# A weight stream of 340 slots: raw buffers dropped, each transfer landing in the ring itself

## The reference

```
# first_block, layer a
h = rms_norm(x, a_norm) @ a_w_in              -> q, k, v, qm, gate
q, k = rope(rms_norm per head of 64)
o  = diff_attention(q, k, v, lam)             # softmax(c=0) - lam * softmax(c=1), 6 heads, causal
om = memory_attention(qm, mem)                # 4 heads over 256 memory rows
x  = x + (cat[rms_norm(o), om] * silu(gate)) @ a_w_out
# first_block, layer b
k, v = split(rms_norm(x, kv_norm) @ w_kv_shared);  q, qm, gate from b_w_in
o  = stick_breaking_attention(q, k, v)        # sigmoids and a running product, 12 heads
x  = x + (cat[o, om] * silu(gate)) @ b_w_out
# second_block, twice
u, v, z_a, c_q, c_kv, k_rope, z_b, x_c, z_c, g_a, g_b, g_c = split(rmsnorm(x) @ w_in)
y_a = gmlp_spatial(u, layernorm(v)) * silu(z_a)
y_b = mla_attention(c_q, c_kv, k_rope) * silu(z_b)          # 8 heads
y_c = rg_lru(conv(x_c)) * silu(z_c)
merged = sig(g_a) * (y_a @ wa) + sig(g_b) * (y_b @ wb) + sig(g_c) * (y_c @ wc)
x = x + rmsnorm(merged @ w_out)
```

## Time and profile before

| | us |
|---|---|
| time, median of 3 runs (2293.51 to 2296.84) | 2294.11 |
| the profiled execution | 2295.78 |
| its span, first to last instruction | 2294.0 |
| PE busy | 2199.1 (96%) |
| DVE busy | 1192.2 (52%) |
| POOL busy | 1151.6 (50%) |
| ACT busy | 936.4 (41%) |

### The profile page before, as it was taken

One profiled execution on the slowest core, in us unless ns is written; L12 is line 12 of the kernel. 1 busy time (PEld: TensorE's weight loads), 2 busy tenths in 40 slices (PEclk: granted clock), 3 DMA queues, 4 the chain that ended last, 5 costly groups with the idle time before them and its releaser, 6 DMA issues.

```text
span 2294.0 us, 27438 instructions
## 1 busy us (share of the span) xinstructions
PE 2199.1 (96%) x10006; PEld 1694.0 (74%) x10006; DVE 1192.2 (52%) x1827; ACT 936.4 (41%) x1591; POOL 1151.6 (50%) x1360
## 2 busy tenths in 40 slices
PE   7999989999899999999999999799999999999998
PEld 5776567775587668888887888576678888877786
DVE  6877875458668341053248843564420432298442
ACT  4546742356444542232234622344532322237322
POOL 4553245642175224565566765263145665575752
PEclk9999999999999999999999999899999999999999
DMA  4222122321132114322232233122133332332321
GB/s 150 78 83 65 38 82 75 110 65 38 37 101 84 55 47 129 101 92 92 83 101 85 90 102 101 55 84 64 35 104 99 94 101 85 93 100 74 110 92 65
DMA packets 53127, 191.45 MB, mean 83 GB/s; under 512 B 6016, under 2 KB 6400, under 8 KB 52480
## 3 DMA queue, kind: packets, MB, share of 16 engines
q1 hardware_dynamic: 51696, 184.44, 25.7%
q10 hardware_dynamic: 1296, 5.24, 0.7%
HBM read 187.56 MB, written 2.10 MB: 83 GB/s over the span
## 4 chain that ended last, share of the span: by engine, by line
PE 76%; DVE 14%; ACT 4%; POOL 2%; issue 2%; DMA 1%; SPq 0%; DVEq 0%; ACTq 0%
PE proj L554 19%; PE proj L556 19%; PE proj L555 19%; PE score L550 4%; PE proj L550 3%; PE stat L550 2%; POOL lower L506 2%; PE turned L550 2%; DVE small L1825 2%; PE mix L550 2%; DVE tmp L1714 1%; PE score L556 1%; PE score L555 1%; PE score L554 1%; DVE h L1719 1%
## 5 line engine op out<-in xcount | busy, mean ns | idle before, releaser
L506 POOL TENSOR_TENSOR lower<-raw_ring,upper 128x256 fp32r<-128x256 f32 x1340 | 1134.9, 881 | 1087.9 <-ACT upper L1214 1087.9
L554 PE MATMUL proj<-h,upper 128*128 128x512 f32 x1424 | 575.5, 404 | 12.7 <-ACT sq L1318 3.1
L1214 ACT ACTIVATE upper<-raw_ring 128x1024 fp32r<-128x1024 f32 x335 | 350.9, 1058 | 529.5 <-PE proj L554 287.8
L556 PE MATMUL proj<-h,lower 128*128 128x512 f32 x1424 | 556.4, 391 | 0.0
L555 PE MATMUL proj<-h,upper 128*128 128x512 f32 x1424 | 555.6, 390 | 0.0
L554 PEld LDWEIGHTS proj<-h,upper 128*128 128x128 f32 x1424 | 268.1, 188 | 77.5 <-issue 5.7
L556 PEld LDWEIGHTS proj<-h,lower 128*128 128x128 f32 x1424 | 267.6, 188 | 57.0
L555 PEld LDWEIGHTS proj<-h,upper 128*128 128x128 f32 x1424 | 268.2, 188 | 51.3 <-issue 1.9
L554 PE MATMUL proj<-y,upper 128*128 128x512 f32 x586 | 234.1, 399 | 13.1 <-ACT qk L1318 5.9
L555 PE MATMUL proj<-y,upper 128*128 128x512 f32 x586 | 229.5, 392 | 0.0
L556 PE MATMUL proj<-y,lower 128*128 128x512 f32 x586 | 229.5, 392 | 0.0
(11 more groups left out here) (461 smaller groups left out, 3494.2 us busy)
## 6 DMA issues: line engine op xcount, KB each, us to landing
raw_ring<-stream SPq DMA_DIRECT2D x335, 512.0 KB, 3.5
landing<-stream SPq DMA_DIRECT2D x5, 512.0 KB, 10.0
x<-x_in SPq DMA_DIRECT2D x4, 512.0 KB, 6.8
rows<-rows_in ACTq DMA_DIRECT2D x2, 1024.0 KB, 5.2
out<-x SPq DMA_DIRECT2D x8, 256.0 KB, 2.5
memraw<-mem_in SPq DMA_DIRECT2D x1, 1024.0 KB, 13.2
memraw<-mem_in ACTq DMA_DIRECT2D x1, 1024.0 KB, 4.8
rot<-tables_in ACTq DMA_DIRECT2D x2, 512.0 KB, 3.2
```

Of the source, the lines that this page charges most:

```text
L506: ins = nc.gpsimd.tensor_tensor(lower[:, p % RING, a:b], slot_source(p)[:, a:b], upper[:, p % RING, a:b].bitcast(FP32), ALU.subtract)
L554: first_ = nc.tensor.matmul(o, lhsT[0], rhs[0], start=start, stop=False)
L556: return first_, nc.tensor.matmul(o, lhsT[1], rhs[0], start=False, stop=stop)
L1214: nc.scalar.activation(upper[:, p % RING, :], slot_source(p), ACT.Copy).then_inc(split_upper, 1)
```

## The change

`raw_ring` and RAWS go. The room (two slots) is given to the rings: `upper` and `lower` have six slots in place of five. Every slot p now lands in `lower[:, p % 6, :]` (named `landing`). SP waits, before it issues slot p, until slot p-6 has been used up; before, it waited for POOL to be done with slot p-2. ACT no longer waits for `slots_used` itself, only for the landing, and copies from the lower half to the upper half; POOL subtracts in place.

```
-RAWS, RING = 2, 5
+RING = 6
...
-    raw_ring = sb("raw_ring", [P, RAWS, SLOT])
     upper = sb("upper", [P, RING, SLOT], FP32R)
     lower = sb("lower", [P, RING, SLOT], FP32R)
     landing = place("landing", cursor[0] - RING * SLOT, [P, RING, SLOT])
...
     def slot_source(p):
-        return landing[:, p, :] if p < RING else raw_ring[:, (p - RING) % RAWS, :]
+        return landing[:, p % RING, :]
     def slot_arrival(p):
-        return (landed[p], 16) if p < RING else (arrived[(p - RING) % RAWS], 16 * ((p - RING) // RAWS + 1))
+        return landed[p % RING], 16 * (p // RING + 1)
...
         for p in range(RING, SLOTS):
-            if p >= RING + RAWS:
-                sp.wait_ge(*slot_ready(p - RAWS))
-            sp.dma_start(slot_source(p), stream[p, :, :]).then_inc(arrived[(p - RING) % RAWS], 16)
+            sp.wait_ge(slots_used, p + 1 - RING)
+            sp.dma_start(slot_source(p), stream[p, :, :]).then_inc(landed[p % RING], 16)
...
             for p in range(fed[0], min(upto, SLOTS)):
                 act.wait_ge(*slot_arrival(p))
-                if p >= RING:
-                    act.wait_ge(slots_used, p + 1 - RING)
                 nc.scalar.activation(upper[:, p % RING, :], slot_source(p), ACT.Copy).then_inc(split_upper, 1)
```

More of the change, by code:

```diff
@@ L300, in build @@
     split_lower = nc.alloc_semaphore("split_lower")
-    arrived = [nc.alloc_semaphore(f"slot_arrived{r}") for r in range(RAWS)]
     landed = [nc.alloc_semaphore(f"slot_landed{p}") for p in range(RING)]
```

## The result

The changed kernel takes 2347.20 us, median of 4 runs (2346.43 to 2348.83), against 2293.86 us for the kernel before (4 runs, 2293.51 to 2296.84): a ratio of 1.0231, 95% interval 1.0218 to 1.0244. It is slower by 53 us. The forecast was 2336, range 2314 to 2350.

What follows compares the result with a forecast made beforehand. PE, busy 96% of the span, was taken to bound the kernel. Losses of 46.7 us less gains of 5.1 gave 41.6 net, hence 2337.4 on the profiled execution and a forecast of 2336 us, range 2314 to 2350.

Steps and rivals of the forecast that it cites:

- The mechanism: Transfer issued at the slot's release, so 80 copies on ACT start up to 3.5 us later, delaying ACT's work behind them.
- the sixth slot gives the copy no head start: In ACT's list the copy is now the next slot's, needing the same release as before; up to 3.5 us later.
- The plain projections: Plain stretches of projections: 3.5 + 1.06 is 4.6, covered by a job ending over 5.2 us after release; cost nothing.
- the differential tiles: Differential attention: square behind the copy comes later, PE's sum loses 2.2 us in each of four tiles; stage total 14.35.
- the fifth: Fifth differential attention tile: square moves from 273.15 to 276.65 and PE's sum loses 3.15 us.
- the three stick-breaking tiles alike: Stick-breaking attention: later sigmoid delays DVE's product, 3.0 us reaching PE in each of three tiles, 9.0; stage total 12.75.
- The rivals: Paid back in attention tiles, 2308.6 (0.10); landing hardly seen (0.06); gain alone, 2289 (0.08); above 2350 (0.06).
- The gains: Shorter ACT waits for raw-buffer transfers give back 5.1 us where PE waited behind them; bounds nothing and 12.
- After the recurrent unit: At 1311.88 ACT's wait for a transfer goes, and PE's wait for the square: 1.7 in both later layers, 3.4 us.
- The gain of 0.7 that I had put at 340: Between 320 and 341 ACT waits for transfers three times; PE waits 6.81 for DVE's x, so only 0.7 us gained.
- The start: First copy out of the raw ring, at 46.18, starts at 48.6 with a take directly behind it: 2.4 us lost.
- The layer norm: Gated unit's layer norm: takes behind the copy move 3.5, DVE's chain ends later, PE's product waits 2.1 per layer, 4.2.

Runs made afterwards that it cites:

- experiment 1: Changed kernel with every later feed on ACT asking for one slot less, so each transfer starts one release ahead of its copy: 2288.82 us, ratio 0.998.
- experiment 2: Kernel before, with SP also waiting until slot p-5 is used up before it issues slot p; nothing lands in place: 2361.28 us, ratio 1.0297.
- experiment 3: Kernel before with SP's additional wait for slot p-5, and each transfer from the eighth slot on bringing only half its columns: 2331.03 us.
- experiment 5: Changed kernel with SP first landing a slot's first 16 columns, then issuing the whole slot, so the landing is later: 2465.13 us.
- Experiments 4 and 6: Changed kernel asking one slot less only behind the attention stages' transposed-probability copies, 2307.67 us; and one slot less everywhere except those copies, 2328.03 us.

## Why the prediction was right, and where it was off

**The mechanism held.** A transfer issued at the release, a copy that waits for it, and ACT's own work behind the copy: experiment 1 removes it and 58 us go, experiment 2 adds it to the kernel before and 68 come (some of them from the waits for POOL named there), experiments 3 and 5 turn it down and up. That the sixth slot gives the copy no head start, since the copy keeps its place in ACT's list, was the step that decided the sign; experiment 1 shows the same slot at work once the list is told to lag.

**The places held.** Experiments 4 and 6 split the loss into the attention tiles and the rest, and the two parts, 39.2 and 18.9 us above experiment 1, make up 58.1 of the changed kernel's 58.4. The plain projections lost nothing at a landing of 3.5 us. In the differential tiles PE's sum behind the square came 1.95 to 2.06 later where 2.2 was forecast, and 3.25 in the fifth for 3.15; in the three stick-breaking tiles alike the delay that reached PE was 2.5 to 2.7 where 3.0 was. The rivals are out: little was paid back in the tiles, and 264 copies saw the landing.

**The gains held in sum, though not each.** After the recurrent unit 3.5 came where 3.4 was forecast. Between 298 and 388 it was 2.6 for 1.7: the queries after the second memory keys gained 4.1, more than I had given them, and 1.4 was lost ahead of them. Of the 4.1, some 2 are the clock: the windows give 0.91 over 370 to 388 in the trace of before and 1.00 over the same matmuls (399 to 413) in the changed kernel. The other 2.1 is PE's wait for POOL there, gone whole, where I had left 1.0 of it. The gain of 0.7 that I had put at 340 did not come.

**The term that was missing is the clock.** The measured shift is 51.0 and the sum was 41.6. PE's busy time rose by 14.4 us, from 2199.1 to 2213.5, for the same matmuls, and by the mean granted clock the core lost 0.017 x 2344.6 = 39.9 us in place of 0.011 x 2294.0 = 25.2, that is 14.6 more. I had forecast the same clock and the same busy time. By stage, in windows over the four attention stages (the row's third number from the end is the granted clock), of the kernel before:

```profile
208.00:298.00 90.00, 85.40 (x416) 51.26 (x417) 74.82 (x193) 63.65 (x173) 21.16 (x28) 1.00 0.16 47
513.00:628.00 115.00, 104.17 (x556) 62.31 (x555) 90.09 (x162) 65.88 (x171) 29.70 (x32) 0.99 0.13 41
723.00:808.00 85.00, 80.30 (x363) 55.99 (x362) 33.64 (x87) 41.77 (x88) 27.11 (x37) 0.98 0.20 62
1508.00:1608.00 100.00, 97.93 (x429) 71.19 (x428) 53.43 (x97) 49.42 (x94) 52.46 (x62) 1.00 0.28 85
```

The same four stages in the trace of the changed kernel:

```profile
216.00:327.00 111.00, 91.03 (x422) 53.52 (x421) 73.05 (x194) 63.57 (x174) 19.73 (x28) 0.97 0.09 29
538.00:668.00 130.00, 109.20 (x555) 63.99 (x554) 90.25 (x162) 66.44 (x174) 31.78 (x32) 0.95 0.10 29
765.00:854.00 89.00, 79.91 (x359) 55.27 (x358) 32.05 (x88) 41.58 (x88) 26.72 (x38) 0.98 0.17 53
1555.00:1661.00 106.00, 100.12 (x423) 71.57 (x423) 54.58 (x97) 48.80 (x94) 53.78 (x62) 0.97 0.23 69
```

In tiles where PE now stood still more often, the granted clock was at its lower level, 1.2 in place of 2.4 GHz, for a part of the time: 3% of 111 us is 3.3 us in the differential stage, some 5% of 130 us less 1% of 115 in the stick-breaking one 5.4, and 3.2 in the fourth layer's attention. Without it these stages would have lost 16.4, 9.6 and 3.5 where the sum had 14.35, 12.75 and 5.05. PE's idle time between the same matmuls grew by 15.4, 10.0 and 3.8 there. So my waits alone came out about 5 us too high in all (36.6 measured without the clock's 14.4), and the clock more than made up for it. That the lower clock goes with the stalls, and is no accident of one run, is borne out by all 4 runs of the changed kernel (0.979 to 0.983, where those of the kernel before have 0.987 to 0.990), by experiment 1 at 0.986 to 0.988 and by experiment 5 at 0.965 to 0.967. How much of each stage's loss is the clock's was only read from these windows, which are rounded to 0.01; no run holds the clock fixed.

**The smaller misses.** The start cost 4.0 for 2.4, of which the clock is part (1.00 before and 0.94 after, in windows over that stretch). The stretch of k in layer a, 1.65, I had at nothing; it holds no new idle time of PE, and the granted clock was 0.96 before and 0.92 after. In the differential stage I had left out PE's waits for the take of `yf`, which grew from 0.8 us to 2.8 in four. The layer norm cost 1.4 per layer for 2.1, since PE's product waited 0.90 and not 2: I had set the end of DVE's chain against the first of the eight matmuls with `gv`, and only the last two needed it. The price of a late landing was taken as linear in the range by halves of a microsecond; experiments 2 and 3 give 30.3 us for 0.9 us of landing, where 25 places would give 22, but 11.7 of the 30.3 are PE's busy time, so the waiting alone came to 18.6. The limit of 4.2 us for the plain projections was too strict: experiment 5, at 5.1, shows hardly any of them losing.

**Landing time and overlap.** The Trainium skill's fit for the other issuing path ("DMA: Bandwidth & Descriptors", section "Anatomy of one DMA — SWDGE (gpsimd) path") gave an estimate of 3.2 us for the landing; the trace after has 3.5 for 340 transfers, so the row decides. For 8 KB, in experiment 5, the page of the profile shows 1.6 us, and for 256 KB, in experiment 3, 2.6. The Trainium skill, "Trainium Kernel Development and Optimization", section "Best Practices", says to double-buffer so that transfer and compute overlap. Taking the buffers away cost 53 us here, as that rule would have it; but experiment 1 has the overlap back without them, by starting the transfer a release ahead of the copy, which takes up the sixth slot of the ring.

## What to carry to other kernels

When a buffer between a transfer and its consumer goes, ask which event starts the transfer now and where in the in-order list its consumer stands; if both hang on the same event, the whole landing time stands ahead of everything behind that consumer, however idle the engine is on average. A slot more in the ring helped only once the consumer's list was told to lag behind it: here the same memory gave +53 us without the lag and -4.5 us with it. And stalls put into PE's stream can cost more than their length: here 36.6 us of them came with 14.4 us of longer matmuls, while the mean granted clock went from 0.989 to 0.983.

## What the hardware showed that was not expected

In two of the traces one DVE instruction took many times its usual length while POOL ran without a break. From experiment 1, DVE and POOL:

```profile
421.65 10.41 DVE L1709 SCALAR_TENSOR_TENSOR tmp<-x,fcol,gate 128x512 f32<-128x512 f32 x1 [18.53 <-PE score L553]
432.10 0.87 DVE L1713 CAST h<-tmp 128x512 fp32r<-128x512 f32 x1
...
417.52 13.99 POOL L503 TENSOR_TENSOR lower<-landing,upper 128x256 fp32r<-128x256 f32 x20 [8.47 <-ACT upper L1209]
```

And from the changed kernel:

```profile
422.98 14.00 POOL L503 TENSOR_TENSOR lower<-landing,upper 128x256 fp32r<-128x256 f32 x20 [11.05 <-ACT upper L1209]
...
429.52 7.74 DVE L1701 TENSOR_TENSOR half_var<-half_var,std 128x256 f32<-128x256 f32 x1 [12.71 <-ACT std L1278]
437.30 0.42 DVE L1702 TENSOR_TENSOR half_var<-half_var,std 128x256 f32<-128x256 f32 x1
```

The first of these operations takes 0.75 to 1.11 us elsewhere in that stretch; here it ended half a microsecond after POOL's row of 20 subtractions, and the second, 0.42 long where it is repeated, ended 0.3 after a row of 20. The Trainium skill, "SBUF — State Buffer", section "SBUF: two separate sides", says that DVE and POOL share a port pair of the on-chip memory, that a DVE instruction with two inputs there and a POOL instruction that reads it contend for it, and that whichever starts first has it for the whole instruction while the other blocks. Here DVE was held over some 14 and 11 of POOL's instructions, which followed each other every 0.70 us. In the kernel before, POOL's runs were broken up by its waits, 8 pieces at most at that place, and no DVE instruction was held so. But an unbroken row alone does not do it: in the changed kernel a row of 24 from 682.58 to 704.75 ran beside DVE instructions with two such inputs, none longer than 1.18 us. Both held ones came after DVE had stood idle for over 12 us; that this is the condition is not shown. In experiment 1 PE's matmuls between 388 and 448 us of before came 4.2 later, and that profiled execution, 2292.82 us, lies 4 above the median of its runs; whether the other runs had no such hold is not known. In the changed kernel that stretch cost nothing. It was seen in these two traces only, and no run was made to bring it about.
